# The opening's scale vector on TensorE with a two-column moving operand, in a two-block fp32 transformer kernel

## What is computed

```
cond = jax.nn.silu(c)                                   # c: (1, 1024)
mod = (cond @ w_ada[l] + b_ada[l]).reshape(b, 6, d)     # w_ada: (1024, 6144)
shift1, scale1, gate1, shift2, scale2, gate2 = [mod[:, i] for i in range(6)]
hn = modulate(rmsnorm(x, norm1_g[l]), shift1, scale1)   # h * (1 + scale) + shift
proj = hn @ w_in[l]
```

## Time and profile before

| what | us |
|---|---|
| median of 3 runs | 2134.18 |
| lowest, highest | 2133.28, 2136.2 |
| the profiled execution's own time | 2133.43 |
| its span, first to last instruction | 2131.6 |
| TensorE busy | 1978.9 |
| VectorE busy | 1288.6 |
| ScalarE busy | 488.7 |
| start of the first projection matmul (L233) | 41.53 |

### The profile page before, as it was taken

How to read it: one execution, slowest core, us unless ns; L and a number is a source line. 1 busy time by engine, 2 the same in 40 slices (tenths; PEclk the granted TensorE clock), 3 DMA queues, 4 the chain that set the end, 5 groups by cost and what they waited for, 6 DMA issues and landing times. The chain is left out here.

```text
span 2131.6 us, 33466 instructions
## 1 busy us (share of the span) xinstructions
PE 1978.9 (93%) x12885; PEld 1850.2 (87%) x12885; DVE 1288.6 (60%) x3222; ACT 488.7 (23%) x1691; POOL 356.8 (17%) x304
## 2 busy tenths in 40 slices
PE   4999998999999999999798778979999999999997
PEld 3886788999999999999686566869999999999996
DVE  5348422999889844443597643223898889644443
ACT  2013302223545300000123112201224445100000
POOL 0000000022323311220003601000022333221120
PEclk8999999999999999999899998999999999999998
DMA  9952235899999999998242030237899999999993
GB/s 352 398 188 80 80 137 198 276 396 382 384 394 381 402 414 414 413 414 330 75 140 78 1 109 0 80 119 270 297 413 371 394 382 394 397 414 413 414 414 145
DMA packets 123310, 604.96 MB, mean 284 GB/s; under 512 B 14540, under 2 KB 16748, under 8 KB 83088
## 3 DMA queue, kind: packets, MB, share of 16 engines
q1 hardware_dynamic: 90784, 379.62, 46.5%
q0 software_dynamic: 30800, 222.07, 26.1%
q10 hardware_dynamic: 1568, 1.12, 0.2%
HBM read 600.14 MB, written 2.62 MB: 283 GB/s over the span
## 5 line engine op out<-in xcount | busy, mean ns | idle before, releaser
L965 PE MATMUL bank<-h,ring 128*128 128x160 f32 x4096 | 570.6, 299 | 0.0
L965 PEld LDWEIGHTS bank<-h,ring 128*128 128x128 f32 x4096 | 559.1, 190 | 0.0
L991 PEld LDWEIGHTS bank<-expert_coef,ring 128*128 128x128 f32 x4096 | 556.7, 190 | 2.7 <-DMA ring<-in_uv 1.7
L991 PE MATMUL bank<-expert_coef,ring 128*128 128x160 f32 x4096 | 557.3, 299 | 1.2 <-DMA ring<-in_uv 1.2
L925 POOL DMA_INDIRECT expert_rows<-in_uv,pair_index x192 | 277.9, 1448 | 1345.4 <-DVEq L1267 533.3
L1124 DVE CUSTOM_DVE_ANT_0 expert_rows<-expert_rows,h_tokens 128x1024 f32<-128x1024 f32 x192 | 234.5, 1221 | 235.6 <-DMA expert_rows<-in_uv,pair_index 235.4
L1131 DVE SCALAR_TENSOR_TENSOR pair_sum<-expert_rows,pair_coef,pair_sum 128x1024 f32<-128x1024 f32 x192 | 245.8, 1280 | 56.5 <-ACT pair_coef L1067 55.0
L1065 ACT ACTIVATE pair_act<-pair_dot 128x1 f32<-128x1 f32 x192 | 38.4, 200 | 540.6 <-DVE pair_dot L1124 540.3
L938 PE MATMUL bank<-h,ring 128*128 128x128 f32 x1024 | 119.1, 281 | 12.7 <-PEq L285 12.7
L938 PEld LDWEIGHTS bank<-h,ring 128*128 128x128 f32 x1024 | 118.6, 197 | 13.4 <-issue 13.4
L1240 DVE TENSOR_SCALAR work<-const,choice 128x128 f32<-128x128 f32 x320 | 102.3, 341 | 0.4 <-DVE picked L1230 0.4
(11 more groups left out here) (362 smaller groups left out, 2147.8 us busy)
## 6 DMA issues: line engine op xcount, KB each, us to landing
ring<-in_ut SPq DMA_DIRECT2D x256, 512.0 KB
ring<-in_uv SPq DMA_DIRECT2D x256, 512.0 KB
ring<-in_dense SPq DMA_DIRECT2D x96, 1024.0 KB
ada<-in_ada POOLq DMA_DIRECT2D x16, 1024.0 KB, 13.1
ada<-in_ada SPq DMA_DIRECT2D x8, 1024.0 KB, 17.6
expert_rows<-in_uv,pair_index POOLq DMA_INDIRECT x192
bias_rows<-proj_t POOLq DMA_DIRECT2D x1, 1536.0 KB, 5.3
x<-in_x_t SPq DMA_DIRECT2D x1, 1024.0 KB, 8.6
```

What stands on the lines that cost most here:

```text
L965: ins = nc.tensor.matmul(k.bank[e % 4][:, 0:DENSE], w[:, kk, :], k.h[:, kk, GATHERED:TOK], start=kk == 0, stop=kk == KD - 1)
L991: ins = nc.tensor.matmul(down_bank(i), w[:, i * P:(i + 1) * P], A[:, e, :], start=False, stop=e == NB - 1, skip_group_check=True)
```

## The change

- Columns 8 to 15 (scale1) leave VectorE. TensorE makes them: the weights of a column are the stationary operand, silu(c) as a column is the moving one. The column is held twice, so that 2 columns move. That is 8 matmuls of 128x128 by 2 columns for each of the 8 columns of `mod`, into bank 7 of PSUM. Four columns are made before the bias rows and four behind them.
- The weights of those chunks are laid out anew in memory (rows on the partitions), and SyncE loads the chunks in the order 0, 4, 1, 5, 2, 6, 3, 7.
- ScalarE's queue loads one small array more (`c_column`), and ScalarE takes its silu.
- The bias rows use banks 1 to 6 instead of 1 to 7.
- VectorE adds the bias to scale1 out of PSUM, and to shift1 as before.
- `h` is written in halves: ScalarE writes the 4 even tiles, VectorE the 4 odd ones.

```diff
 def ada_finish(k, dve, ch, j0, j1):
     dve.wait_ge(k.ada_done.sem, k.ada_done.at(j1))
+    if j0 == 0:
+        made = k.bank[7][:, 0:2 * KD].rearrange("p (j n) -> p j n", n=2)[:, :, 0]
+        ch(k.nc.vector.tensor_tensor(k.mod[:, KD:j1], made, k.vec("b_ada")[:, KD:j1], ALU.add))
+        j1 = KD
     ch.then(k.nc.vector.tensor_tensor(k.mod[:, j0:j1], k.mod[:, j0:j1], k.vec("b_ada")[:, j0:j1], ALU.add))
...
-                for c in range(ADA_SLOTS):
+                for c in range(ADA_SLOTS // 2):
                     ada_load(k, sp, c)
+                    ada_load(k, sp, ADA_SLOTS // 2 + c)
...
-                for kk in range(KD):
+                for kk in range(0, KD, 2):
                     nc.scalar.activation(k.h[:, kk, 0:TOK], sq[:, kk, :], ACT.Identity,
                                          scale=k.gain[:, 0, kk:kk + 1], bias=k.mod[:, kk:kk + 1])
...
+                def modulation(j):
+                    c = j // 2
+                    if j % 2 == 0:
+                        pe.wait_ge(k.ada_loaded[c], 16)
+                    w = k.ada[:, c, :, :].rearrange("p a n -> p (a n)").rearrange("p (k n) -> p k n", k=KD)
+                    for kk in range(KD):
+                        ins = nc.tensor.matmul(k.bank[7][:, 2 * (j - KD):2 * (j - KD) + 2], w[:, kk, (j % 2) * P:(j % 2 + 1) * P],
+                                               column[:, kk, :], start=kk == 0, stop=kk == KD - 1)
+                    ins.then_inc(k.ada_done.sem, 1)
+
+                pe.wait_ge(k.squared.sem, k.squared.at(1))
+                for j in range(KD, KD + 4):
+                    modulation(j)
                 pe.wait_ge(k.qk_ready.sem, k.qk_ready.at(1))
                 for h in range(HEADS):
...
+                for j in range(KD + 4, ADA_FIRST):
+                    modulation(j)
...
-                for j in range(8, ADA_FIRST):
-                    ada_column(k, dve, j)
                 dve.wait_ge(k.const_dma, 48)
                 ada_finish(k, dve, ch, 0, ADA_FIRST)
...
+                dve.wait_ge(k.weights_ready.sem, k.weights_ready.at(1))
+                dve.wait_ge(k.sq_ready.sem, k.sq_ready.at(2))
+                for kk in range(1, KD, 2):
+                    nc.vector.tensor_scalar(k.h[:, kk, 0:TOK], sq[:, kk, :], k.gain[:, 0, kk:kk + 1], k.mod[:, kk:kk + 1],
+                                            ALU.mult, ALU.add)
```

More of the change, by code:

```diff
@@ L356, in opening @@
         rs = ctx.enter_context(nc.sbuf_tensor(k.name("rs"), [P, 2, TOK], F32))
+        column = ctx.enter_context(nc.sbuf_tensor("c_column", [P, KD, 2], F32))
         x = k.x[:, :, META:]
@@ L371, in _ @@
                 act.dma_start(k.cond[:, :], bass.AP(args["c_row"].tensor, 0, [[0, P], [1, D]])).then_inc(k.cond_dma, 16)
+                act.dma_start(column[:, :, :], args["c_column"]).then_inc(k.cond_dma, 16)
                 act.dma_start(k.onehot[:, :], args["onehot"]).then_inc(k.cond_dma, 16)
@@ L376, in _ @@
                 act.dma_start(k.x[:, :, 0:META], args["meta_t"]).then_inc(k.const_dma, 16)
-                act.wait_ge(k.cond_dma, 48)
+                act.wait_ge(k.cond_dma, 64)
                 nc.scalar.activation(k.cond[:, :], k.cond[:, :], ACT.Silu).then_inc(k.act_step.sem, 1)
+                nc.scalar.activation(column[:, :, :], column[:, :, :], ACT.Silu).then_inc(k.squared.sem, 1)
                 nc.scalar.activation(rel[:, :, :], k.rel[:, :].unsqueeze(2).broadcast_to([BUCKETS, HEADS, P]), ACT.Copy)\
@@ L384, in _ @@
                     act.wait_ge(k.trans_ready.sem, k.trans_ready.at(h + 1))
-                    nc.scalar.activation(row[:, h, :], k.bank[1 + h % 7][:, 0:3 * P], ACT.Copy).then_inc(k.bias_rows.sem, 1)
+                    nc.scalar.activation(row[:, h, :], k.bank[1 + h % 6][:, 0:3 * P], ACT.Copy).then_inc(k.bias_rows.sem, 1)
                 act.wait_ge(k.sq_ready.sem, k.sq_ready.at(2))
                 act.wait_ge(k.weights_ready.sem, k.weights_ready.at(1))
-                for kk in range(KD):
+                for kk in range(0, KD, 2):
                     nc.scalar.activation(k.h[:, kk, 0:TOK], sq[:, kk, :], ACT.Identity,
@@ L405, in _ @@
                 ins.then_inc(k.tile_ready.sem, 1)
+                def modulation(j):
[10 more added lines that the diff above has]
+                    modulation(j)
                 pe.wait_ge(k.qk_ready.sem, k.qk_ready.at(1))
                 for h in range(HEADS):
-                    pe.wait_ge(k.bias_rows.sem, k.bias_rows.at(h - 6))
-                    nc.tensor.matmul(k.bank[1 + h % 7][:, 0:3 * P], rel[:, h, :], k.onehot[:, :], start=True, stop=True)\
+                    pe.wait_ge(k.bias_rows.sem, k.bias_rows.at(h - 5))
+                    nc.tensor.matmul(k.bank[1 + h % 6][:, 0:3 * P], rel[:, h, :], k.onehot[:, :], start=True, stop=True)\
                         .then_inc(k.trans_ready.sem, 1)
+                for j in range(KD + 4, ADA_FIRST):
+                    modulation(j)
             @block.vector
@@ L433, in _ @@
                     .then_inc(k.weights_ready.sem, 1)
+                dve.wait_ge(k.weights_ready.sem, k.weights_ready.at(1))
[3 more added lines that the diff above has]
+                                            ALU.mult, ALU.add)
+    k.squared.advance(1)
     k.sq_ready.advance(2)
@@ L2236, in layout @@
     b = np.concatenate([a["ssm_b_re_2"][0].transpose(0, 2, 1), a["ssm_b_im_2"][0].transpose(0, 2, 1)], 2)
+    ada = np.ascontiguousarray(a["w_ada"][0].T.reshape(ADA_TILES, P, D).transpose(1, 0, 2))
+    for c in range(KD // 2, KD):
+        ada[:, 2 * c:2 * c + 2] = a["w_ada"][0][:, 2 * c * P:2 * (c + 1) * P].reshape(KD, P, 2 * P).transpose(1, 0, 2).reshape(P, 2, D)
     return {
         "dense": dense,
-        "ada": np.ascontiguousarray(a["w_ada"][0].T.reshape(ADA_TILES, P, D).transpose(1, 0, 2)),
+        "ada": ada,
+        "c_column": np.ascontiguousarray(np.repeat(a["c"].reshape(KD, P).T[:, :, None], 2, 2)),
         "c_row": np.ascontiguousarray(a["c"].reshape(1, D)),
```

## The result

The changed kernel takes 2145.6 us in the median of 6 runs (2143.14 to 2148.09), the kernel before 2133.73 in 6 runs beside it (2128.72 to 2136.2). The ratio is 1.006, with a 95% interval of 1.0044 to 1.0075: 11.9 us slower. The forecast was 2147.9, the range 2139 to 2152. The profiled execution has its own time of 2144.85 and a span of 2142.8; of before they were 2133.43 and 2131.6.

A forecast was written before the change was run, and what follows sets the result against it. The opening was taken as bound by VectorE's column chain. 18.3 + 4.2 at full clock, then 5.7 + 10.4 + 13.4 at half, + 3.2 gave 55.2, 13.7 us later: 2147.9 from the 2134.2 median, range 2139 to 2152.

The forecast's parts named there:

- The bound: Opening: a VectorE column chain delays h and all behind it; without eight columns VectorE's normalized x ends at 32.3.
- Start of TensorE's part: Opening: TensorE starts the scale1 matmuls at 18.3 us, when the sum of squares is done.
- Full-clock price: Scale1 on TensorE: 0.112 us per record at full clock, 14.3 us for 128 records, set by weight loads.
- Rival 3: Two-column records cost clearly less than L484's, so VectorE sets the end: projections 6.0 us earlier, 2128.2; 3 in 100.
- Fall of the clock: TensorE's light matmuls in the opening let its clock fall to 0.50 at 22.5 us, between 20 and 24.4.
- Rival 1: Clock stays at 1.00 because TensorE is busy without a gap: first projection at 41.3, 2134.0, no change; 9 in 100.
- Slow price: Scale1 on TensorE at clock 0.50: 0.21 us per record, between 0.112 and 0.21.
- Rival 2: Clock falls but weight loads keep 0.112 us: first projection at 46.3, 4.8 us later, 2139.0; 5 in 100.
- Bias rows: Bias matmuls between the two scale1 halves: 5.42 us at full clock grows to 10.4 at half clock.
- The tail: From the end of scale1 through gain and halved h writes to the first projection: 3.2 us, where it was 5.1.
- The sum: Opening: first projection at 55.2 us against 41.5, 13.7 us later.

The follow-up runs named there:

- e4: Changed kernel with all eight scale1 columns behind the bias rows, instead of four before and four behind: 2148.05 us, ratio 1.0083 to the kernel before.
- e6: Changed kernel with only two scale1 columns on TensorE, ahead of the bias rows, the other 14 on VectorE: 2129.09 us against 2131.1 before, ratio 0.9993.
- e3: Changed kernel plus 25 dense matmuls nobody reads, between scale1 columns and behind every second bias matmul: 2152.17 us, ratio 1.0098 to the kernel before.
- e5: e3 with one dense matmul behind every bias matmul instead of every second, 29 unread matmuls in all: 2152.14 us, ratio 1.0112 to the kernel before.
- e9: Changed kernel with 128 identical moving columns instead of 2 and one bias matmul behind each scale1 column: 2133.54 us, ratio 1.0008 to the kernel before.
- e8: Changed kernel with 64 identical moving columns instead of 2, same matmuls and order: 2142.34 us, ratio 1.004 to the kernel before.
- e10: Changed kernel with four scale1 columns on TensorE, 128 moving columns, two bias matmuls behind each, twelve on VectorE: 2128.39 us against 2131.77 before, ratio 0.9984.
- e1: Kernel before with only the h writes halved between ScalarE and VectorE, all 16 columns on VectorE: 2130.02 us against 2131.61 before, ratio 0.9989.

## Why the prediction was right

**The bound.** VectorE's chain ended the opening, and with TensorE on it everything behind moved. Right: of 12.7 us at the first projection 11.9 came out in the median. VectorE was done at 33.0 (30.74 + 2.29), not at 32.3, which cost nothing, since it then waited for TensorE.

**Start of TensorE's part.** 18.3 forecast, 17.0 measured. The sum of squares took 5.22 us where it had taken 6.53: the clock rose earlier in it in this execution. I had left that moment open by an us or two.

**Full-clock price.** 0.112 per record by L484, and 29 records in 3.0 us are that, with those cut by the edges. Six columns fewer gave nothing, as forecast; Rival 3 had no ground.

**Fall of the clock.** 22.5 forecast, between 20 and 24.4; 21.9 measured, and 21.6 in e4 and e6. That it fell is the mechanism, and it came true; that it fell within an us of my 22.5 is in part luck, since the moment scatters. The ground for it was thin too: in the earlier trace rows the clock fell when TensorE had been idle for 0.7 us, and behind L484 after a gap, so those rows alone could not tell light work from idleness. The changed kernel and e4 can, since TensorE was busy there up to the fall. Rival 1 fell with it, as did a reading of the Trainium skill's sentence on activity ("TensorE: Matmul & The Clock Gate", Part 1: The HAM clock gate) by which being busy is enough: in e4 TensorE is busy without a gap for 27 us at 0.50.

**Slow price.** 0.21 per record forecast, bounds 0.112 and 0.21. Measured: the second half took 13.81 us for 64 records, the last of which is 0.352 long, so (13.81 - 0.35) / 63 = 0.214. That is the upper bound; L938 in the earlier trace rows was the right neighbour. Rival 2 fell. The rule of the Trainium skill ("TensorE: Matmul & The Clock Gate", LDWEIGHTS), 107 ns for 128 columns, agrees with the 0.112 at full clock and not with 0.214 at half; the measurement decides. The sum by it would have been 2139.0, 6.6 us short.

**Bias rows.** 10.4 forecast, 10.5 from start to start (26.68 to 37.21).

**The tail.** 3.2 forecast; 51.02 to 54.19 is 3.17. VectorE's four writes took 1.38, less than ScalarE's 2.07, and lie beside them.

**The sum.** 55.2 forecast for the first projection, 54.19 measured; the earlier start (1.3) outweighs the second half, which took 0.4 more than summed. The time came 2.3 us under the forecast, 1.0 of it here, the rest in the stretch behind the first projection, where kernels that are equal there differ by more. That the time came this close is therefore in part luck. The projections also stayed at 0.50 for 1.9 us longer than I had assumed; by the earlier trace rows that is worth about 1 us, which that stretch does not show.

What I got wrong came behind the prediction. In the experiments that were to hold the clock it did not hold to the end in two, and their first projections came 16.6 us (e3) and 7.7 us (e5) later than summed. In e9 it held, and the opening still came 3.7 us late, by the price of changing between two kinds of matmul and by ScalarE's queue.

## What to carry to other kernels

A matmul with two moving columns costs its full weight load, and in these runs a stretch of them let TensorE's clock fall to half while every busy row still says 100%: such work has to be priced at both levels of the clock (here 0.112 and 0.213 us per fp32 record), and with what comes behind it. If a vector has to be made on TensorE, try it with more moving columns, even identical ones: up to 128 they cost nothing per record here (0.112 in e8 and e9), and the clock held longer. How much of e9's 10.5 us is the width and how much the order was not separated; the width of 64 alone gave 3.5 in the profile. And move only so much that the receiving engine still ends before the giving one: with two or four of the eight columns the opening ended 1.1 and 2.1 us earlier than with none (e6 and e10 against e1, profiles alone), with all eight at two moving columns it lost 12.7.

## What the runs showed of the hardware that I had not expected

The load of 128 weight columns itself is slower at 1.2 GHz, not only the stream: 0.112 us per record with two moving columns in the first half of the changed kernel, 0.213 in the second.

The moment at which the clock changes is not the program's: the same 16 records of the sum of squares, with starts 0.2 us apart, took 5.2 us in the changed kernel (from 11.94) and 6.7 us in e6 (12.14 to 18.82). And the same bias rows right behind them kept the clock to their end before, but not in e4, where it fell at 21.6, nor in e1, whose opening is the same up to there:

```profile
17.60:22.20 4.60, 4.60 (x16) 2.67 (x16) 4.49 (x7) 2.27 (x7) 0.00 (x0) 1.00 1.01 404
22.40:23.50 1.10, 1.10 (x2) 0.01 (x1) 1.10 (x3) 0.61 (x2) 0.00 (x0) 0.50 0.95 383
```

Other such falls in a kernel may be part of its scatter of some us; no run here separates that.

32 rows by 384 columns, a nearly pure stream, don't hold the clock reliably: it fell in them in e1, e4 and e8. Nor did they bring it back where they began at 0.50, over 10.6 us in the changed kernel and in e6.
